# Inverse levels on 32-column operands, and a new order of the recurrent stage, in a hybrid decoder layer on one core

## The reference

```python
def gdn_chunked(q, k, v, g, beta, s0):
    ...
    G = jnp.cumsum(gc, axis=-1)
    decay = jnp.exp(jnp.where(incl, G[..., :, None] - G[..., None, :], -jnp.inf))
    kb = kc * bc[..., None]
    lower = jnp.where(strict, jnp.einsum('bhntd,bhnsd->bhnts', kb, kc) * decay, 0.0)
    a_mat = lower + jnp.eye(CHUNK, dtype=lower.dtype)
    rhs = jnp.concatenate([vc * bc[..., None], kb * jnp.exp(G)[..., None]], axis=-1)
    sol = lax.linalg.triangular_solve(a_mat, rhs, left_side=True, lower=True, unit_diagonal=True)
    ...
def gdn_recurrent(q, k, v, g, beta, s0):
    def step(s, inp):
        s = jnp.exp(gt)[..., None, None] * s
        u = bt[..., None] * (vt - jnp.einsum('bhd,bhde->bhe', kt, s))
        s = s + kt[..., None] * u[..., None, :]
        return s, jnp.einsum('bhd,bhde->bhe', qt, s)
```

## Time and profile before

| | |
|---|---|
| median of 3 runs | 1975.34 us (1969.19 to 1978.47) |
| the profiled execution | 1973.66 us |
| its span in the profile | 1972.0 us |
| PE busy | 1850.0 us (94%) |
| DVE busy | 1152.9 us (58%) |
| ACT busy | 763.8 us (39%) |
| POOL busy | 244.1 us (12%) |
| mean granted clock of PE | 0.977 |

### The profile page before, as it was taken

One profiled execution on the slowest core, in us unless ns is written; L12 is line 12 of the kernel. 1 busy time (PEld: TensorE's weight loads), 2 busy tenths in 40 slices (PEclk: granted clock), 3 DMA queues, 4 the chain that ended last, 5 costly groups with the idle time before them and its releaser, 6 DMA issues.

```text
span 1972.0 us, 34279 instructions
## 1 busy us (share of the span) xinstructions
PE 1850.0 (94%) x13811; PEld 1744.9 (88%) x13811; DVE 1152.9 (58%) x1588; ACT 763.8 (39%) x772; POOL 244.1 (12%) x226
## 2 busy tenths in 40 slices
PE   5999999858996989999999999999999999999996
PEld 3999999856886989988764999999999999999996
DVE  5888444571765647755545656666544466665443
ACT  1554544332224343334443334444333344443332
POOL 6000000000532530000000540000000000000331
PEclk9999999978998999999999999999999999999998
DMA  5555555413204556788685468888555789985452
GB/s 163 171 170 171 171 171 171 131 44 96 86 1 140 171 196 202 255 276 277 232 298 185 154 186 231 240 257 240 156 175 176 209 232 253 253 219 169 157 184 88
DMA packets 413654, 362.57 MB, mean 184 GB/s; under 512 B 11343, under 2 KB 373838, under 8 KB 412774
## 3 DMA queue, kind: packets, MB, share of 16 engines
q1 hardware_dynamic: 386198, 336.53, 55.7%
q10 hardware_dynamic: 27392, 25.17, 4.0%
HBM read 345.67 MB, written 16.19 MB: 184 GB/s over the span
## 4 chain that ended last, share of the span: by engine, by line
PE 85%; DVE 8%; ACT 3%; issue 2%; POOL 1%; DMA 0%; DVEq 0%; POOLq 0%; ACTq 0%; SPq 0%
PE ps L423 66%; PE ps L443 9%; DVE w_lo L407 2%; PE ps L1169 1%; PE ps L836 1%; ACT w_hi L400 1%; PE ps L1177 1%; PE ps L952 1%; PE ps L984 1%; PE ps L1138 1%; PE ps L1038 1%; PE ps L1029 0%; DVE cacc L536 0%; DMA raw<-in_ffn_w_up_dram 0%; DVE act_lo L1641 0%
## 5 line engine op out<-in xcount | busy, mean ns | idle before, releaser
L400 ACT ACTIVATE w_hi<-raw 128x2048 fp32r<-128x2048 f32 (+1 forms) x289 | 519.8, 1799 | 926.7 <-PE ps L423 801.5
L407 DVE TENSOR_TENSOR w_lo<-raw,w_hi 128x2048 fp32r<-128x2048 f32 (+1 forms) x289 | 629.6, 2179 | 319.5 <-ACT w_hi L400 316.3
L423 PE MATMUL ps<-act_hi,w_lo 128*128 128x264 f32 x2576 | 740.1, 287 | 12.9 <-DVE w_lo L407 9.7
L423 PE MATMUL ps<-act_lo,w_hi 128*128 128x264 f32 x2576 | 732.3, 284 | 0.0
L423 PE MATMUL ps<-act_hi,w_hi 128*128 128x264 f32 x2576 | 732.0, 284 | 0.0
L423 PEld LDWEIGHTS ps<-act_hi,w_lo 128*128 128x128 f32 x2576 | 487.6, 189 | 16.7 <-issue 8.1
L423 PEld LDWEIGHTS ps<-act_lo,w_hi 128*128 128x128 f32 x2576 | 487.9, 189 | 0.6
L423 PEld LDWEIGHTS ps<-act_hi,w_hi 128*128 128x128 f32 x2576 | 485.3, 188 | 0.0
L423 PE MATMUL ps<-ff_hi,w_lo 128*128 128x264 f32 x704 | 201.3, 286 | 4.3 <-DVE ff_lo L559 4.3
L423 PE MATMUL ps<-ff_hi,w_hi 128*128 128x264 f32 x704 | 200.8, 285 | 0.0
L423 PE MATMUL ps<-ff_lo,w_hi 128*128 128x264 f32 x704 | 200.2, 284 | 0.0
(11 more groups left out here) (369 smaller groups left out, 1936.3 us busy)
## 6 DMA issues: line engine op xcount, KB each, us to landing
raw<-in_w_in_dram SPq DMA_DIRECT2D x56, 1024.0 KB, 6.7
raw<-in_ffn_w_gate_dram SPq DMA_DIRECT2D x44, 1024.0 KB, 5.8
raw<-in_ffn_w_up_dram SPq DMA_DIRECT2D x44, 1024.0 KB, 10.4
raw<-in_ffn_w_down_dram SPq DMA_DIRECT2D x32, 768.0 KB, 4.6
raw<-in_ffn_w_down_dram SPq DMA_DIRECT2D x32, 640.0 KB, 5.8
raw<-in_w_out_dram SPq DMA_DIRECT2D x16, 1024.0 KB, 7.7
raw<-in_xa_w_q_dram SPq DMA_DIRECT2D x16, 1024.0 KB, 7.2
raw<-in_xa_w_k_dram SPq DMA_DIRECT2D x16, 1024.0 KB, 6.3
```

The costliest lines, as they stand in the source:

```text
L400: act.activation(w_part(ph, w_hi[b]), raw_part(ph, r, half), ACT.Copy)\
L407: dve.tensor_tensor(w_part(ph, w_lo[b]), raw_part(ph, r, half), w_part(ph, w_hi[b]), ALU.subtract)\
L423: mm = pe.matmul(ps[:, acc(ph, u), 0:ph.cols], w[b][:, k, :], v[:, kk + k, 0:ph.cols], start=first and k == 0 and m == 0, stop=last and k ...
```

## The change

The shapes of the small levels, and the order on all engines of the recurrent stage:

- Levels 2 to 5 work on packed operands: `Tc`, `Yc` (128 x 16 units x 32) hold only the 32x32 blocks on the diagonal, stacked in partitions. Each product has 32 columns instead of 128. DVE copies the new blocks into `Tc` by a mask and turns four 32-row blocks per group back into U; at level 5 a whole transpose makes `Tm` again.
- POOL makes `Ld`, Lt inside the diagonal blocks, once per group instead of `Bt` for every level. The sign is moved into `Lt` (`NBETA`), and DVE's subtractions become masked copies.
- PE's order is skewed: Y of step n, then U times Y of step n - 1, through all levels, written out by hand for the last two.
- The turns of `cv` go between the GLA state products. The GDN state products and the GLA sums go between the pair products. POOL adds the two squares, the sum is copied to `gla`, and logarithm and exponential follow after the last decays.
- `sample_outputs` goes behind all levels, `scale_keys` in four parts into the last two, ACT's first split of `w_out` ahead of the squares. Two memsets and two selects are added to the constants at the start.

```diff
+            m = 1 << SQUARE_LEVELS
+            pool_link(pool, pool.memset(levels[:, 0, :], 0.0))
+            pool_link(pool, pool.memset(v, 1.0))
+            pool_link(pool, pool.affine_select(out=v, ...))
+            pool_link(pool, pool.affine_select(out=v, ...))
             pool.memset(pre[:, :, 0:CW - 1], 0.0).then_inc(consts_ready, 1)
...
+            W(pool, "norm_sq", 1)
+            pool.tensor_tensor(nsq[:, 0:8:2, :], nsq[:, 0:8:2, :], nsq[:, 1:8:2, :], ALU.add).then_inc(N["gdn_qkm"], 1)
             for g in range(4):
                 W(pool, "gdn_lt", g + 1)
-                pool.tensor_tensor(Bt[:, 4 * g:4 * g + 4, :], Lt[:, 4 * g:4 * g + 4, :], ...)
+                pool.tensor_tensor(Ld[:, 4 * g:4 * g + 4, :], Lt[:, 4 * g:4 * g + 4, :],
+                                   diag[:, :].unsqueeze(1).broadcast_to([P, 4, P]), ALU.mult).then_inc(N["gdn_bt"], 1)
...
+                for b in (2 * g, 2 * g + 1):
+                    for h in range(GH):
+                        n = h * NB + b
+                        mm = pe.matmul(ps[0:GH * NB, 5, 0:GDV], gqe[:, n, :], gst[:, b, h, :], ...)
...
+            W(pe, "gdn_ktok", 4)
+            W(pe, "gdn_vb", 4)
+            pairs(0)
+            pe.wait_ge(rows_copied, 1)
+            for e in range(2):
+                mm = turn(ps[:, 5, 256 + e * 32:256 + (e + 1) * 32], grow[:, e * P:(e + 1) * P])
...
+            on_state(0)
+            on_state(1)
+            pe.wait_ge(gla_done, 1)
+            pairs(1)
+            on_state(2)
+            norm_sum(0)
+            on_state(3)
+            norm_sum(1)
+            W(pe, "gdn_lt", 1)
+            pairs(2)
+            on_state(4)
+            norm_sum(2)
+            on_state(5)
+            norm_sum(3)
+            W(pe, "gdn_lt", 2)
+            pairs(3)
+            on_state(6)
+            on_state(7)
...
+            def narrow_y(n):
+                W(pe, "inv_ready", n + 1)
...
+                for i in range(4):
+                    mm = pe.matmul(ps[:, Y_BANK[n % 3], i * BW:i * BW + BW], Ld[:, 4 * g + i, :], Tc[:, 4 * g + i, :], ...)
+            def narrow_t(n):
+                W(pe, "y_copied", n + 1)
...
+                    mm = pe.matmul(ps[:, T_BANK[n % 3], i * BW:i * BW + BW], U[:, 4 * g + i, :], Yc[:, 4 * g + i, :], ...)
+            last = 4 * (SQUARE_LEVELS - 1) - 1
+            for n in range(last + 1):
+                narrow_y(n)
+                if n:
+                    narrow_t(n - 1)
+                if n == 2:
+                    sample_rows()
+            whole_y(SQUARE_LEVELS + 1, 0)
+            narrow_t(last)
+            whole_y(SQUARE_LEVELS + 1, 1)
+            whole_y(SQUARE_LEVELS + 1, 2)
+            both(0)
+            whole_y(SQUARE_LEVELS + 1, 3)
+            both(1)
+            both(2)
+            whole_y(LEVELS - 1, 0)
+            both(3)
+            whole_y(LEVELS - 1, 1)
+            whole_y(LEVELS - 1, 2)
+            last_u(0)
+            whole_y(LEVELS - 1, 3)
+            for g in range(1, 4):
+                last_u(g)
...
+            rstd_gla = nsq[:, 1:8:2, :]
+            act.activation(rstd_gla, rstd_gla, ACT.Ln, ...).then_inc(N["norm_rb"], 1)
+            W(act, "norm_rb", GH + 1)
+            act.activation(rstd_gla, rstd_gla, ACT.Exp, scale=-0.5).then_inc(N["norm_rb"], 1)
             act.wait_ge(srow_done, 1)
...
+            split(PH["w_out"], 0, 0)
+            W(act, "gdn_sval", 1)
             for g in range(2):
                 W(act, "gdn_e4", 2 * g + 1)
                 act.activation(osq[:, 4 * g:4 * g + 4, :], cv[:, 4 * g:4 * g + 4, :], ACT.Square).then_inc(N["norm_sq"], 1)
-            for u in range(2):
-                split(PH["w_out"], 0, u)
+            split(PH["w_out"], 0, 1)
...
+            def bases(g):
+                W(dve, "gdn_lt", g + 1)
+                link(dve.tensor_copy(ug, b3(ident[:, :], 4)))
+                link(dve.copy_predicated(ug, b3(levels[:, 1, :], 4).bitcast(U32), lt))
+                for b in range(P // BW):
+                    at = slice(BW * b, BW * b + BW)
+                    ins = dve.transpose(Tc[at, 4 * g:4 * g + 4, :], U[at, 4 * g:4 * g + 4, at])
+                ins.then_inc(N["inv_ready"], 1)
...
+            masks(0)
+            decays(1)
+            bases(0)
+            for g in range(1, 4):
+                masks(g)
+                if g < 3:
+                    decays(g + 1)
+                bases(g)
...
+            for n in range(4 * (LEVELS - 2)):
+                l, g = 2 + n // 4, n % 4
+                W(dve, "tyuy_done", n + 1)
...
+                if l <= SQUARE_LEVELS:
+                    link(dve.copy_predicated(Tc[:, 4 * g:4 * g + 4, :], ...))
+                    for b in range(P // BW):
+                        at = slice(BW * b, BW * b + BW)
+                        ins = dve.transpose(U[at, 4 * g:4 * g + 4, at], Tc[at, 4 * g:4 * g + 4, :])
+                    if l == SQUARE_LEVELS:
+                        link(ins)
+                        ins = dve.transpose(units(Tm, g), units(U, g))
+                    ins.then_inc(N["inv_ready"], 1)
+                elif l == SQUARE_LEVELS + 1:
+                    dve.copy_predicated(tm, b3(levels[:, 0, :], 4).bitcast(U32), heads_of(b0))
+                    dve.copy_predicated(um, mask, heads_of(b0 + 1)).then_inc(N["inv_ready"], 1)
+                    if g >= 2:
+                        scale_keys(g - 2)
+                else:
+                    dve.copy_predicated(um, mask, heads_of(LAST_U[g])).then_inc(N["inv_ready"], 1)
+                    if g < 2:
+                        scale_keys(g + 2)
+            sample_outputs()
```

More of the change, by code:

```diff
@@ L47 @@
 SQUARE_LEVELS = 5
+BW = 32
+Y_BANK = (0, 2, 3)
+T_BANK = (5, 4, 6)
+WHOLE_Y = (1, 2, 3, 0)
+BOTH = (6, 4)
+LAST_U = (6, 7, 4, 5)
 UNIT_CREDIT = 2
@@ L118, in build @@
         rstd = place("rstd", [P, TT], F32)
+        SQ0 = Here.at
         sq = place("sq", [P, 2, TT], F32)
@@ L987, in on_state, with norm_sum, pairs @@
                     mm.then_inc(srow_done, 1)
[L989 to L995, removed]
+            def norm_sum(t):
+                W(pe, "gdn_qkm", 1)
+                if t:
+                    W(pe, "norm_rb", t)
+                pe.matmul(ps[:, 5, 0:TT], ones[:, :], nsq[:, 2 * t, :], start=True, stop=True).then_inc(N["norm_sum"], 1)
+            def pairs(g):
                 b0 = 4 * (g % 2)
@@ L1005, in _ @@
                 mm.then_inc(N["gdn_pair"], 1)
[L1006 to L1014, removed]
-            W(pe, "gdn_sx", 1)
-            for m in range(2):
-                pe.matmul(ps[:, 1, m * 64:(m + 1) * 64], ones[0:NB, :],
-                          sdiag[:, m, :, :].rearrange("p b h -> p (b h)"), start=True, stop=True)
@@ L1812, in _, with four, decays @@
             ins.then_inc(N["gla_out"], 1)
+            for g in range(4):
+                W(dve, "gdn_turned", g + 1)
+                dve.tensor_copy(vb[:, 4 * g:4 * g + 4, :], heads_of(2 * (g % 2) + 1)).then_inc(N["gdn_vb"], 1)
+            def four(v):
+                return v.rearrange("p (h c) d -> p h c d", c=2)
+            def decays(g):
+                W(dve, "gdn_pair", g + 1)
+                for n in range(4):
+                    ins = dve.tensor_scalar(QK[:, 4 * g + n, :], ps[:, 4 * (g % 2), n * P:(n + 1) * P],
+                                            sm(GC)[:, 2 * g + n // 2, n % 2:n % 2 + 1], 0.0, ALU.subtract, ALU.min)
+                ins.then_inc(N["gdn_dmin"], 1)
@@ new lines, in masks @@
+            def masks(g):
+                W(dve, "gdn_dexp", g + 1)
+                b0 = 4 * (g % 2)
+                lt, qk = Lt[:, 4 * g:4 * g + 4, :], QK[:, 4 * g:4 * g + 4, :]
+                if g == 0:
+                    W(dve, "gla_smm", NB)
+                for n in range(4):
+                    beta = sm(BETA)[:, 2 * g + n // 2, n % 2:n % 2 + 1]
+                    less = sm(NBETA)[:, 2 * g + n // 2, n % 2:n % 2 + 1]
+                    at_n = slice(n * P, (n + 1) * P)
+                    dve.scalar_tensor_tensor(out=lt[:, n, :], in0=ps[:, b0 + 2, at_n], scalar=less, in1=qk[:, n, :],
+                                             op0=ALU.mult, op1=ALU.mult)
+                    ins = dve.scalar_tensor_tensor(out=qk[:, n, :], in0=ps[:, b0 + 3, at_n], scalar=beta, in1=qk[:, n, :],
+                                                   op0=ALU.mult, op1=ALU.mult)
+                ins.then_inc(N["gdn_lt"], 1)
@@ L1813, in _ @@
+            decays(0)
             W(dve, "gla_turned", 3)
```

295 lines of the change are left out of this document (146 added, 149 removed).

## The result

| | before | after |
|---|---|---|
| median | 1973.53 us (1969.19 to 1978.47, 4 runs) | 1986.53 us (1984.82 to 1987.21, 4 runs) |
| ratio | | 1.0066, 95% interval 1.0052 to 1.0080 |
| span of the profiled execution | 1972.0 us | 1984.5 us |
| mean granted clock of PE | 0.977 | 0.966 |

The changed kernel is slower by 0.66%, 13 us.

A forecast was written before the change was run, and what follows sets the result against it. PE, holding 85% of the chain of waits, was taken as the bound. Gains of 14.4 and 1.8 less 1.2 lost made 15.0 us, so a median of 1960 us, likely 1956 to 1965, range 1954 to 1986.

The forecast's parts named there:

- The price of a narrow product: PE's small levels: a 32-column product costs 0.112 us, the same as a whole one; bounds 0.056 and 0.112.
- rival 1: PE's clock halves over the narrow stretch, a step takes 3.58 us, time 1985 (1980 to 1990); chance 0.22.
- Front of the stage: Recurrent stage up to the last GDN state product: ends at 507.6 instead of 515.1, 7.5 us gained, without PE waits.
- rival 4: The order fails: PE waits among the pair products, 7.5 us less gain, 1968; chance 0.19 together with rival 3.
- First narrow steps: Behind the last pairs: PE waits 2.5 us for ACT, Y of step 3 starts at 515.7; 2.5 us given back.
- Steps 3 to 15: Small levels: PE's 1.79 us per step exceeds DVE's 1.45; last narrow product ends at 540.0, 9.2 us gained so far.
- Levels 6 and 7: Last two levels: PE ends at 557.4, DVE at 559.0, with key scaling at 1.2 us per half (upper bound 2.3).
- f1: Step behind the levels: its first product starts at 559.1 instead of 573.50, 14.4 us gained.
- f1 to `w_out`: From step f1 to the first `w_out` product: ACT's first split moves into its wait before the squares, 1.8 us gained.
- The start: Kernel start: two memsets and two selects on POOL delay PE's first work, 1.2 us lost (bounds 0.9 and 1.4).

The follow-up runs named there:

- late: Changed kernel with ACT's logarithm and exponential of the GLA norms moved behind the level steps, products still 32 columns: 1982.34 us, ratio 1.0050.
- wide: Changed kernel with every small-level product streaming its packed 32 columns four times, so 128 columns; weights, loads, order and waits kept: 1962.18 us, ratio 0.9936.
- wide_state: The kernel wide with the GDN state products put back in one block behind the last pair products: 1962.05 us, ratio 0.9947.
- half64: The kernel wide, but packed columns streamed twice instead of four times, 64 columns per product: 1987.14 us, ratio 1.0071.
- t_wide: Changed kernel with only the T products (U times Y) streaming 128 columns, Y products staying at 32: 1987.52 us, ratio 1.0076.
- wide_late: Changed kernel with the edits of both wide and late: 128 streamed columns, GLA norms behind the level steps: 1961.29 us, ratio 0.9941.
- best: The kernel wide with POOL's level masks built behind its start signal, and step f1's first half waiting only for groups 0 and 1: 1957.51 us, ratio 0.9926.

## Why the prediction was wrong

**The price of a narrow product** is the step that failed. The forecast priced it at 0.112 us "the same as a whole one", from rows at full clock. The rows at full clock were right: in the kernel late, eight narrow instructions at 510.73 start 0.89 us before the next eight, 0.111 each. At the low clock the price was in the rows too, 0.213 us in the changed kernel against the 0.22 of the earlier trace rows. The number of streamed columns set neither; that the load of the 128 weight columns does is the forecast's reading, which fits these figures, but no run here changed the weights. What failed is the clock at which the price was taken: the narrow stretch ran at 0.50, not at 1.00, and its 0.213 us instead of 0.112 is what cost the 24 to 26 us. The only rows about the clock and narrow operands showed 32-column *weights* with 128 columns streamed, which held 1.00 for 14 us. The change makes the opposite, 128-column weights with 32 streamed, and the stretch with them ran at 0.50 for 58 us. The forecast named this asymmetry in rival 1 and gave it 0.22; the row that it put against the rival was of another form and should have carried little.

**Rival 1** was right in each of its numbers: a step at 1.2 GHz is 3.42 us (forecast 3.58), the gain is turned into a loss, and the time is 1986.5 (forecast 1985). In its argument one of two reasons falls: the wait ahead of the stretch is neither needed (late) nor enough (wide). Of TensorE: Matmul & The Clock Gate, Part 1, in the Trainium skill, the forecast had cited that the clock goes by how busy the array was. By that, the window of 58 us is a surprise if busy is read as instructions issued without a gap: PE was busy in 57.63 of 58.00 us at 0.50. The runs with 32, 64 and 128 columns show that what each product streams counts, while the advice of this page of the Trainium skill, to avoid idle gaps, would not have helped here: late had none ahead of its fall. The section LDWEIGHTS of the same page of the Trainium skill lets a load's time go by its weight columns, as columns divided by 1.2 in ns, 107 for 128. The 111 ns here at the full clock agree with that, for 32 and for 128 streamed columns; the 213 ns at the low clock are twice as much.

**The rest of the sum** can be read in wide, where the clock is out of it. From there, term by term:

- *Front of the stage.* 7.5 us were forecast. From GLA to the last state product it is 50.1 us instead of 55.7, so 5.6. The order held, without a wait of PE among the pairs (busy in 28.69 of the 28.69 us from the first pair product on in wide); rival 4 was false. Every term was a little too small: GLA state products and turns took 21.1 us (forecast 20.7), the pairs 11.3 (10.8), the GDN state products in their six pieces 14.7 (14.1), the GLA sums 2.4 (1.8).
- *First narrow steps.* PE's wait for ACT was 2.15 us, forecast 2.5. The forecast's own terms add up to 511.5 for ACT, not to 511.9, and behind the wait stand three groups of eight and not two; the two slips nearly cancel. But Y of step 3 starts at 518.3 in wide, not at 515.7. That is the lateness of the last state product (510.3 for 507.6), of which 0.5 is that execution's own later start of the stage (460.5 for 459.98).
- *Steps 3 to 15.* A step is 1.79 us of PE in wide, as forecast, and DVE's 1.59 (0.30 and four turns at 0.31, forecast 0.4 and 0.26) lies below it. The last T ends at 543.5, forecast 540.0. Besides the 2.6 above, one group of eight products (0.9) was left out of the count behind Y of step 15.
- *Levels 6 and 7.* From the last T to f1 it is 19.3 us, forecast 19.1. DVE's half of the keys took 1.20 us with POOL idle, the value chosen; the upper bound of 2.3 was not needed.
- *f1.* Together that is 562.8 instead of 559.1. The whole gain of order and waits from GLA to f1 is 11.4 us (114.1 less 102.7), not 14.4.
- *f1 to `w_out`.* 1.8 us forecast, 1.8 measured in the changed kernel, and 1.8 lost again when the split alone was put back.
- *The start.* 1.2 us forecast, 1.1 measured at the first tile (41.1 against 40.0). At 397 us 0.5 of it were left (397.30 for 396.79).
- *What carries the 11.4.* The interleaved state products 2.9 to 4.6 (without and with the fall of the clock in wide_state), the sample outputs behind the levels 1.6; the remainder, some 5 to 7 us, belongs to the skewed order of the small and last levels with its packed operands together, which no run here took apart. The forecast had put 5.0 us (7.5 less the 2.5 of the wait) on the front, and of what the interleaving brings there, 6.9, ACT's tables, which the block had covered, take 2.2.
- *The packed operands* by themselves did not make DVE's step cheaper. Before, a group of a small level cost DVE 0.65 us of subtraction and 0.71 of turn, a new one every 1.32 us; packed it is 0.30 and 1.25. ACT's copy fell from 0.60 to 0.27 us, and POOL was spared `Bt`, 20 products of 1.48 us from 515 to 575, for four of 1.33 on `Ld`. Both old rates, 1.32 and 1.48 us a group, are below PE's 1.79. As an estimate from these, operands of 128 columns in the skewed order would have kept up with PE as well; no run tried it.

Taken together, the sum without the clock would have been about 1962. The forecast's 1960 with 1956 to 1965 was good for a kernel that streams 128 columns, and not for this one.

## What to carry to other kernels

Cutting the columns that a product streams saved no time here, 0.111 us with 32 as with 128, and it took the clock from the whole stretch. The packed operands saved ACT and POOL time, cost DVE a little, and suited PE only when it streamed them four times through a broadcast view. Before packing operands, ask which engine the stage waits for: here it was PE, for which packing brought nothing. When pricing a change that makes many operands smaller, take the price at both clock levels, and ask of the row that argues for the full clock whether it has the same form on both sides, weights and streamed columns. When PE's busy share rises and its waits fall while the time grows, look at the granted clock by windows before any wait.

## What the runs showed of the hardware

- Products of 128x128 fp32 weights that streamed 32 columns ran at 1.2 GHz for 58 us, with PE busy in 57.63 of 58.00 us. Ahead of the fall PE had issued them without a gap (late). With 64 columns (half64), or with 128 on every second group of eight (t_wide), it was 0.50 too (53.8 and 54.2 us); with 128 on all (wide) it was 1.00 throughout 29.2 us, though PE had waited 2.08 us just ahead.
- At 1.2 GHz such an instruction took 0.213 us with 32 columns, at 2.4 GHz 0.111 us with either 32 (late) or 128 (wide).
- In the changed kernel the last narrow products end near 568.8 us, and the whole ones behind them still ran at the low clock until 571.4 us.
- Whether a wait is followed by the low clock differed: 3.16 us before (3.4 us at 0.50) and 1.26 us in wide_late (3.5 us at 0.51) were, 2.08 us in wide was not. Behind the wait of 3.1 us at GLA it was 0.50 until 466.1 us in wide, and 1.00 in wide_state, where the code up to there is the same.
- A DVE turn of 32 partitions and 128 columns took 0.30 us (0.31 from start to start), where a whole 128x512 one took 0.711: four of them, which together cover 128 partitions and 128 columns, cost 1.25 us, more than the whole turn with four times the columns.
- With POOL's signal out of the way, PE's first three waits are for transfers, and end at 5.9, 8.7 and 14.8 us in the kernel best. PE's start 5.3 us earlier brought 1.4 us at the first tile.
